# Latent attention in a float32 trunk: another PSUM bank for the rotary queries, and the values' high and low weights in one 512-column product

## The reference

```python
h = rmsnorm(x, norm_g)
q_lat, kv_lat, k_rope, gate = split(h @ w_in)
q = (rmsnorm(q_lat) @ w_q_up).reshape(B, S, 16, 128 + 64)
q_nope, q_rope = q[..., :128], apply_rope(q[..., 128:], cos, sin)
kv = (rmsnorm(kv_lat) @ w_kv_up).reshape(B, S, 16, 128 + 128)
k_nope, v = kv[..., :128], kv[..., 128:]
k_rope = apply_rope(k_rope, cos, sin)
s = (q_nope . k_nope + q_rope . k_rope) * scale, causal
o = softmax(s) . v
y = (o * silu(gate)) @ w_out
```

## Time and profile before

| | us |
|---|---|
| median of three runs | 801.30 |
| profiled execution, its own time | 801.27 |
| its span from first to last instruction | 799.5 |
| TensorE matmul busy | 789.3 (99%) |
| VectorE busy | 477.9 (60%) |
| ScalarE busy | 418.2 (52%) |
| GpSimd busy | 121.3 (15%) |
| mean granted clock of TensorE, share of full speed | 0.997 |

### The profile page before, as it was taken

How to read it: one execution, slowest core, us unless ns; L and a number is a source line. 1 busy time by engine, 2 the same in 40 slices (tenths; PEclk the granted TensorE clock), 3 DMA queues, 4 the chain that set the end, 5 groups by cost and what they waited for, 6 DMA issues and landing times.

```text
span 799.5 us, 11521 instructions
## 1 busy us (share of the span) xinstructions
PE 789.3 (99%) x3976; PEld 669.7 (84%) x3976; DVE 477.9 (60%) x734; ACT 418.2 (52%) x647; POOL 121.3 (15%) x213
## 2 busy tenths in 40 slices
PE   9999999999999999999999999999999999999996
PEld 7888888888888888888888888888888999988885
DVE  5567766655454454557545655355667888865554
ACT  6654444446455454654445645345566666654452
POOL 7411223102011030230000010050000000000222
PEclk9999999999999999999999999999999999999998
DMA  9874765666667666644667666566545445435512
GB/s 316 284 225 134 196 172 161 184 167 174 184 162 204 176 196 183 201 140 137 199 193 210 178 184 191 158 186 185 159 136 165 117 147 197 153 124 184 196 55 106
DMA packets 78317, 140.29 MB, mean 175 GB/s; under 512 B 9272, under 2 KB 14560, under 8 KB 78144
## 3 DMA queue, kind: packets, MB, share of 16 engines
q1 hardware_dynamic: 76496, 137.34, 57.6%
q10 hardware_dynamic: 1584, 1.84, 0.7%
q0 software_dynamic: 192, 0.53, 0.2%
HBM read 137.06 MB, written 2.62 MB: 175 GB/s over the span
## 4 chain that ended last, share of the span: by engine, by line
PE 88%; issue 8%; DVE 1%; POOL 1%; ACT 0%; POOLq 0%; ACTq 0%; DVEq 0%
PE ps L1416 22%; PE ps L1418 22%; PE ps L1417 22%; PE ps L1794 4%; PE ps L1795 2%; PE ps L1438 2%; PE ps L1880 1%; PE ps L1843 1%; PE ps L1842 1%; PE ps L1841 1%; PE ps L1590 1%; PE ps L1473 1%; POOL even L585 1%; PE ps L1855 1%; PE ps L1552 1%
## 5 line engine op out<-in xcount | busy, mean ns | idle before, releaser
L963 DVE TENSOR_TENSOR w_lo<-raw,w_hi 128x1024 fp32r<-128x1024 f32 x239 | 299.5, 1256 | 259.6 <-ACT w_hi L615 259.1
L615 ACT ACTIVATE w_hi<-raw 128x1024 fp32r<-128x1024 f32 x236 | 249.8, 1059 | 272.1 <-PE ps L1418 267.9
L1416 PE MATMUL ps<-w_hi,a_parts 128*128 128x512 f32 x868 | 341.5, 393 | 0.0
L1418 PE MATMUL ps<-w_hi,a_parts 128*128 128x512 f32 x868 | 338.2, 390 | 0.0
L1417 PE MATMUL ps<-w_lo,a_parts 128*128 128x512 f32 x868 | 337.9, 389 | 0.0
L1418 PEld LDWEIGHTS ps<-w_hi,a_parts 128*128 128x128 f32 x868 | 162.9, 188 | 34.5
L1416 PEld LDWEIGHTS ps<-w_hi,a_parts 128*128 128x128 f32 x868 | 163.0, 188 | 33.0 <-issue 0.3
L1417 PEld LDWEIGHTS ps<-w_lo,a_parts 128*128 128x128 f32 x868 | 163.1, 188 | 32.4
L1794 PE MATMUL ps<-a_parts,w_hi 128*128 128x512 f32 x160 | 56.7, 398 | 1.7 <-DVE nmx L1285 1.7
L1795 PE MATMUL ps<-a_parts,w_lo 128*128 128x256 f32 x160 | 44.6, 279 | 0.0
L1794 PEld LDWEIGHTS ps<-a_parts,w_hi 128*128 128x128 f32 x160 | 30.0, 188 | 8.6 <-DVE nmx L1285 2.0
(11 more groups left out here) (273 smaller groups left out, 780.1 us busy)
## 6 DMA issues: line engine op xcount, KB each, us to landing
raw<-in_w_in_even SPq DMA_DIRECT2D x111, 512.0 KB, 3.8
raw<-in_w_in_odd SPq DMA_DIRECT2D x48, 512.0 KB, 3.7
raw<-in_w_out_even SPq DMA_DIRECT2D x32, 512.0 KB, 3.8
raw<-in_w_out_odd SPq DMA_DIRECT2D x32, 512.0 KB, 3.7
raw<-in_w_kv_up SPq DMA_DIRECT2D x16, 512.0 KB, 3.7
raw<-in_w_q_up SPq DMA_DIRECT2D x16, 384.0 KB, 3.3
xs<-in_x SPq DMA_DIRECT2D x6, 256.0 KB, 8.4
even<-in_final_norm SPq DMA_DIRECT2D x1, 1024.0 KB, 6.9
```

The source lines that it names most:

```text
L615: return a.activation(w_hi[:, ring, 0:w], raw[:, s, 0:w], ACT.Copy)
L963: return v.tensor_tensor(w_lo[:, ring, 0:w], raw[:, s, 0:w], w_hi[:, ring, 0:w].bitcast(F32), ALU.subtract)
L1416: m.matmul(acc, a_hi[:, k, tok], hi, start=first, stop=False)
L1418: ins = m.matmul(acc, a_lo[:, k, tok], hi, start=False, stop=last)
```

## The change

It has two parts. First, from the second turn on the rotary queries go to bank 2 and the first head's keys to bank 7 (`rope_and_keys`); the wait for `nmx_ready` moves from ahead of the rotary queries to ahead of the keys. Second, the high and low weight parts are one tensor, `w_parts`, so that one product of 512 columns multiplies the high tokens by both. The sums of high and low stand side by side in PSUM: tile 0 in bank 3, tile 1 in the bank that held the rotary queries (so TensorE now waits for `rope_out` ahead of the values). ScalarE copies both banks to `v_halves` in SBUF, and GpSimd adds the halves of each tile to make `v_tok`. New waits: ScalarE for the last turn's sum (`v_ready`) ahead of its copies, TensorE for `v_ready` ahead of the mixing, and in the first turn TensorE for ScalarE's first copy ahead of the scores of tile 0.

```diff
@@ -94,6 +94,11 @@
...
+def rope_and_keys(first):
+    return (7, (2, 5)) if first else (2, (7, 5))
 def levels_done(lev):
@@ -127,8 +132,8 @@
...
         raw = sb("raw", [P, RAW, PK * CW])
-        w_hi = sb("w_hi", [P, RING, PK * CW], F32R)
-        w_lo = sb("w_lo", [P, RING, PK * CW], F32R)
+        w_parts = sb("w_parts", [P, RING, 2, PK * CW], F32R)
+        w_hi, w_lo = w_parts[:, :, 0, :], w_parts[:, :, 1, :]
@@ -161,6 +166,7 @@
...
         v_tok = [even[:, 7424 + 512 * i:7936 + 512 * i].rearrange("p (t n) -> p t n", t=T) for i in range(2)]
+        v_halves = work[:, 0:1024].rearrange("p (t a n) -> p t a n", t=T, a=2)
         cos4 = even[:, 8448:8704].rearrange("p (t b n) -> p t b n", t=T, b=4)
@@ -260,6 +266,7 @@
...
         rope_seq, qr_taken, qr_ready, kt_done = (sem(n) for n in ("rope_seq", "qr_taken", "qr_ready", "kt_done"))
+        v_ready = sem("v_ready")
         rope_rest_ready, q_rest_ready, k_rest_ready, q_out, rope_out = (
@@ -583,10 +590,14 @@
...
                 g.tensor_scalar(part, part, rstd[:, 4 + n:5 + n], None, ALU.mult).then_inc(lat_ready, 1)
-            with pool.Fori(0, PAIRS) as p:
-                pool.wait_ge(evac_d, p * 2 + (C_MLA + 1))
-                g.tensor_tensor(q_rot, q_cos, q_sin, ALU.add).then_inc(rope_seq, 1)
+            with pool.Fori(0, PAIRS // 2) as i:
+                for par in range(2):
+                    pool.wait_ge(evac_d, i * 4 + (C_MLA + 1 + 2 * par))
+                    g.tensor_tensor(q_rot, q_cos, q_sin, ALU.add).then_inc(rope_seq, 1)
+                    pool.wait_ge(evac_a, i * 4 + (C_MLA + 2 + 2 * par))
+                    g.tensor_tensor(v_tok[par], v_halves[:, :, 0, :], v_halves[:, :, 1, :], ALU.add).then_inc(v_ready, 1)
             pool.wait_ge(fin_landed, 16)
@@ -893,6 +904,7 @@
...
                 nxt = (FULL,) * 4 if last else UP
+                rope_bank, key_banks = rope_and_keys(first)
@@ -904,14 +916,14 @@
...
                 act.wait_ge(piece_used, pieces_through(p * 2 + C_MLA, "up"))
-                a.activation(rope_rest, ps[:, 7, T * P:], ACT.Copy).then_inc(rope_rest_ready, 1)
+                a.activation(rope_rest, ps[:, rope_bank, T * P:], ACT.Copy).then_inc(rope_rest_ready, 1)
                 a.activation(qn_rest, ps[:, 0:2, T * P:], ACT.Copy).then_inc(q_rest_ready, 1)
...
                     for h in range(2):
-                        a.activation(kn_rest[:, h, :], ps[:, 2 + 3 * h, T * P:], ACT.Copy).then_inc(k_rest_ready, 1)
+                        a.activation(kn_rest[:, h, :], ps[:, key_banks[h], T * P:], ACT.Copy).then_inc(k_rest_ready, 1)
@@ -922,7 +934,10 @@
...
                 act.wait_ge(piece_used, pieces_through(p * 2 + (C_MLA + 1), "up"))
-                a.activation(v_tok[par].rearrange("p t n -> p (t n)"), ps[:, 3, :], ACT.Copy).then_inc(evac_a, 2)
+                if not first:
+                    act.wait_ge(v_ready, p)
+                for t, bank in ((1, rope_bank), (0, 3)):
+                    a.activation(v_halves[:, t, :, :], ps[:, bank, :].rearrange("p (a n) -> p a n", a=2), ACT.Copy).then_inc(evac_a, 1)
                 if not first:
@@ -1287,6 +1302,7 @@
...
                 nxt = (FULL,) * 4 if last else UP
+                rope_bank, key_banks = rope_and_keys(before is None)
@@ -1299,7 +1315,7 @@
...
                 dve.wait_ge(rope_rest_ready, p + 1)
-                v.tensor_tensor(q_rope, ps[:, 7, 0:T * P], rope_rest, ALU.add).then_inc(rope_out, 1)
+                v.tensor_tensor(q_rope, ps[:, rope_bank, 0:T * P], rope_rest, ALU.add).then_inc(rope_out, 1)
                 dve.wait_ge(rope_out, p + 1)
@@ -1310,7 +1326,7 @@
...
                     dve.wait_ge(k_rest_ready, p * 2 + (h + 1))
-                    ins = v.tensor_tensor(kn_t[:, T * P * h:T * P * h + T * P], ps[:, 2 + 3 * h, 0:T * P], kn_rest[:, h, :], ALU.add)
+                    ins = v.tensor_tensor(kn_t[:, T * P * h:T * P * h + T * P], ps[:, key_banks[h], 0:T * P], kn_rest[:, h, :], ALU.add)
                 ins.then_inc(evac_d, 1)
@@ -1809,15 +1826,15 @@
...
                         pe.wait_ge(table_out, 2)
-                    elif j == 0:
-                        pe.wait_ge(nmx_ready, p)
                     for k in ks:
                         hi, lo = (query_rope(w, j)[:, k % 2, :, :, :].rearrange("p a h n -> p (a h n)") for w in (w_hi, w_lo))
-                        ins = exact(ps[:, 7, :], hi, lo, k, k == 0, k == 3)
+                        ins = exact(ps[:, rope_bank, :], hi, lo, k, k == 0, k == 3)
                     ins.then_inc(piece_used, 1)
...
                 pe.wait_ge(evac_d, p * 2 + C_MLA)
+                if not first:
+                    pe.wait_ge(nmx_ready, p)
@@ -1829,18 +1846,19 @@
...
                         for k, hi, lo in kv_piece(j):
-                            ins = exact(ps[:, 2 + 3 * h, :], hi[:, h, 0:DH], lo[:, h, 0:DH], k, k == 4, k == 7)
+                            ins = exact(ps[:, key_banks[h], :], hi[:, h, 0:DH], lo[:, h, 0:DH], k, k == 4, k == 7)
                 ins.then_inc(kt_done, 1)
...
                     pe.wait_ge(my_ready, p * 4 - 4)
+                pe.wait_ge(rope_out, p + 1)
                 for j in (2, 3):
                     for k, hi, lo in kv_piece(j):
-                        for t in range(T):
-                            o, tok = ps[:, 3, 256 * t:256 * t + 256], slice(P * t, P * t + P)
-                            m.matmul(o, a_hi[:, k, tok], hi[:, :, DH:], start=k == 4 and t == 0, stop=False, skip_group_check=True)
-                            m.matmul(o, a_hi[:, k, tok], lo[:, :, DH:], start=False, stop=False, skip_group_check=True)
-                            ins = m.matmul(o, a_lo[:, k, tok], hi[:, :, DH:], start=False, stop=k == 7, skip_group_check=True)
+                        both = w_parts[:, j, :, CW * (k % PK):CW * (k % PK) + CW].rearrange("p a (h n) -> p a h n", h=2)
+                        for t, bank in ((0, 3), (1, rope_bank)):
+                            o, tok = ps[:, bank, :], slice(P * t, P * t + P)
+                            m.matmul(o, a_hi[:, k, tok], both[:, :, :, DH:], start=k == 4, stop=False, skip_group_check=True)
+                            ins = m.matmul(o[:, 0:2 * DH], a_lo[:, k, tok], hi[:, :, DH:], start=False, stop=k == 7, skip_group_check=True)
                     ins.then_inc(piece_used, 1)
@@ -1857,6 +1875,7 @@
...
                 p = i * 2 + par
+                pe.wait_ge(v_ready, p + 1)
                 for h in range(2):
@@ -1868,7 +1887,7 @@
...
-            def scores(i, par):
+            def scores(i, par, first=False):
@@ -1876,6 +1895,8 @@
...
                     o = ps[:, 7 - t, 0:2 * n]
+                    if t == 0 and first:
+                        pe.wait_ge(evac_a, p * 2 + (C_MLA + 1))
                     for h in range(2):
@@ -1907,7 +1928,7 @@
...
             pe.wait_ge(krl_ready, 4)
-            scores(0, 0)
+            scores(0, 0, first=True)
             turn_of(0, 1, 0, first=True)
```

## The result

| | before | after |
|---|---|---|
| median of the runs, us (the six of before include the three told above) | 801.25 (6 runs, 801.01 to 801.69) | 805.68 (6 runs, 805.16 to 805.94) |
| profiled execution, us | 801.27 | 805.54 |
| span, us | 799.5 | 803.8 |
| TensorE, VectorE, ScalarE, GpSimd busy, us | 789.3, 477.9, 418.2, 121.3 | 791.5, 482.9, 419.9, 138.9 |
| granted clock of TensorE, share of full speed | 0.997 | 0.998 |

The ratio after to before is 1.0055, with a 95% interval of 1.0045 to 1.0065: slower by 4.4 us, at the same clock. The forecast was 805.6.

The account below looks back on a forecast made before the run. TensorE bound the kernel (88% of the chain, turns of 13.93 us), VectorE's loop only 0.16 shorter. First turn +1.12, six turns +2.6, last sum +0.59: together +4.3 on 801.27, so 805.6 us; range 802.0 to 809.8.

Parts of the forecast that it names:

- GpSimd's sum: GpSimd's two-input SBUF sum, taken as 1.27 us, excludes VectorE's low parts and takes turns with them: +0.59 a turn.
- The loop: VectorE and ScalarE from one rotary queries' sum to the next: 13.77 us before, 14.36 with GpSimd's sum.
- First turn: GpSimd's sum falls among back-to-back low parts before nmx and holds VectorE up by 1.12 us; second turn's split ends 613.28.
- the rival with no cost: Low parts keep their second input, GpSimd's sum starts at the masking, loop stays under 13.84: 800.4 us, chance 0.16.
- Six turns: From the second turn's rotary split to the last turn's, VectorE's loop sets the turn: 6 × (14.36 − 13.93) = +2.6 us.
- GpSimd first: Rival: GpSimd's sum starts before VectorE's low part, which waits the full 1.12; loop 14.89, 809.3 us, chance 0.30.
- The stall: TensorE's 1.83 us wait for nmx in the second turn goes; at most 0.38 gained before it waits for qr_ready.
- The products: TensorE's values: a 512- and 256-column pair, 0.347 us, replaces three 256-column products, 0.359; 0.09 a turn, 0.74 in all.
- ScalarE's copy: A second values' copy of 0.60 us a turn makes the last high part up to 0.32 late for VectorE, costing nothing.

Follow-up runs that it names:

- the kernel with the sum of one column: Changed kernel with GpSimd's sum over one column of each tile instead of 256, all copies, banks, products and waits kept; 800.43 us, ratio 0.9990.

## Why the prediction was right

**GpSimd's sum** was the term that decides, and its steps stand. The sum waits for the low part in progress, then the next low part waits for it: predicted +0.59, measured 1.78 − 1.22 = +0.56. The loop was put at 14.36 and is 14.35. That a blocked instruction goes on 0.15 us before the other's recorded end holds too (629.14 + 0.56 = 629.70 against 627.53 + 2.31 = 629.84, that is 0.14).

**First turn**: 1.12 predicted. The two small low parts lose 1.10, and the split of the second turn ends at 613.21 for the 613.28 forecast. The low parts did not hold their second input from one instruction to the next: GpSimd got in between two that were queued back to back. That was the rival with no cost, and it is refuted there.

**Six turns** at +0.43 and the last one's +0.59: the loop was longer by 14.35 − 13.93 = 0.42. Over the six turns together the rotary sum of VectorE fell back by 2.74 us (86.20 from the second turn to the last, 83.46 before) for 2.6, since the first of them took 13.78 before and not 13.93; the last sum cost 0.56. TensorE's start of the projection moved by 4.34 us for 4.3.

**GpSimd first** had 0.30. It did not happen in the changed kernel, by 0.02 to 0.06 us in each turn, inside the "within 0.1" that the prediction named. The prediction had no row that could settle so small a distance, so that 805.6 came and not 809.3 is in part luck; the price of either order was worked out. Why the distance stays the same from turn to turn no run tested. My reading is that the values, and with them the sum, follow VectorE's last turn, since TensorE waits for it in every turn; in the run with the sum on the kernel before the distance did not settle. There it fell on the other side in three turns, at 14.87 for the forecast 14.89. That kernel has one copy less ahead of the sum, but the old banks and products too, so which of them moves the sum is open.

**The stall**: at most 0.38 of its 1.83 us was to come back; with the banks alone 0.41 did, and the changed kernel had none, since VectorE's 1.1 was on top. The new banks did save another loss, though: in the run with the sum on the kernel before, which has the old ones, the same 1.10 of the first turn grew to 2.1 (15.31 − 13.21).

**The products**: 0.347 a pair was predicted, and (625.71 − 622.93) / 8 = 0.348 came out, 0.012 less than the three products of the earlier trace rows. The 512-column product whose columns lie in four runs costs nothing extra.

**ScalarE's copy**: up to 0.32 late, hidden beside the sum. Alone it made the low part 0.14 late, and the time did not move by more than the interval.

One thing the prediction had only half: it hid the products' gain behind VectorE only because of the sum, and its no-cost rival counted it for six turns in full, 0.92 us with the stall's 0.38, at 800.4. In the kernel with the sum of one column TensorE did come 0.98 earlier by the last transposes, but the projection only 0.56, since VectorE's loop ends the layer even without the sum's blocking. That its median is 800.43 agrees with the rival's number more than with its working.

## What to carry to other kernels

Before giving the idle GpSimd a sum from SBUF, look at what VectorE does in that very stretch: beside an instruction with two SBUF inputs the two took turns here, beside the masking, which reads PSUM, they did not. If VectorE's loop is within a few tenths of the bound, hold the sum back to a stretch of PSUM reads, or cut it into pieces that fit the gaps; 4.9 us came back that way here for one more wait, and 4.0 for the two pieces. A stall that goes is worth only the distance to the next wait of the same chain, so look for that wait before counting it.

## What the runs showed of the hardware that was not expected

- A longer record can be the cheaper one: GpSimd's two pieces show 3.36 us and cost VectorE nothing, one sum of 2.31 us cost it 0.56.
- VectorE's negative maximum reads one small SBUF tensor (128x4) and took 240 ns on average beside GpSimd's held-back sum, 170 without it. In one place, beside a second piece, it took 0.46 us. Masking instructions in the same stretch, with one input in PSUM, kept their 0.42.
- In the run with the sum on the kernel before, whether GpSimd started 0.07 us ahead of VectorE's low part or 0.04 behind it was worth 14.87 − 14.34 = 0.53 us a turn.
